# Latent attention rebuilt: keys and values first, two heads per unit in paired tiles, queries grouped by part

## The reference, cut to what matters

```
cq, ckv, k_rope = split(h @ w_down, [256, 384])            # 256 | 128 | 32 columns
q  = (rms_norm(cq)  @ w_uq ).reshape(b, s, 16, 64 + 32)    # q_nope, q_rope
kv = (rms_norm(ckv) @ w_ukv).reshape(b, s, 16, 64 + 64)    # k_nope, v
q_rope, k_rope = apply_axial_rope(...)                     # latent tokens only
s = (q_nope . k_nope + q_rope . k_rope) * 96 ** -0.5       # 16 heads, 256 queries, 512 keys
y = (softmax(s) @ v) @ w_o
```

## Time and profile before

| quantity | value |
|---|---|
| median of 3 runs | 3352.78 us (3351.43 to 3356.87) |
| the profiled execution, on the device | 3355.39 us |
| its span, first to last instruction | 3354.1 us |
| TensorE busy | 3137.0 us, 94% of the span |
| VectorE busy | 1747.7 us, 52% |
| ScalarE busy | 1449.1 us, 43% |
| GpSimd busy | 995.2 us, 30% |
| mean granted TensorE clock | 0.974 of full speed |

### The profile page before, as it was taken

The page is one execution under the profiler, slowest core; times in us unless marked ns, Lnnn a source line. Parts: engine busy times, 40 slices in busy tenths (PEclk is TensorE's granted clock), DMA queues, the critical chain, the costliest instruction groups (busy, mean ns, idle before and its releaser), DMA issues.

```text
span 3354.1 us, 50677 instructions
## 1 busy us (share of the span) xinstructions
PE 3137.0 (94%) x21050; PEld 2666.3 (79%) x21050; DVE 1747.7 (52%) x3034; ACT 1449.1 (43%) x2412; POOL 995.2 (30%) x440
## 2 busy tenths in 40 slices
PE   5989998999899998889979989999999999999899
PEld 3767776776677775569979977877999978779899
DVE  3353333655543333756556646555456556654565
ACT  3442222444432223544454445555444446554443
POOL 0312222110212222123433432333444433434433
PEclk8999999999899999999989989999999999999999
DMA  8345444332355552125525532333545433334454
GB/s 289 121 143 163 157 159 137 126 101 89 121 173 171 168 171 90 38 63 178 193 91 164 188 116 89 101 101 94 166 143 183 157 115 96 99 101 151 151 177 151
DMA packets 469299, 459.97 MB, mean 137 GB/s; under 512 B 9040, under 2 KB 467664, under 8 KB 469072
## 3 DMA queue, kind: packets, MB, share of 16 engines
q1 hardware_dynamic: 465760, 453.32, 42.4%
q10 hardware_dynamic: 3312, 3.42, 0.3%
HBM read 455.66 MB, written 1.05 MB: 136 GB/s over the span
## 4 chain that ended last, share of the span: by engine, by line
PE 77%; DVE 11%; ACT 7%; issue 3%; POOL 1%; DMA 1%; ACTq 0%; DVEq 0%; POOLq 0%
PE bank L399 22%; PE bank L400 21%; PE bank L401 21%; PE bank L443 3%; ACT wh L346 3%; DVE wl L362 2%; DVE hl L707 1%; PE bank L1474 1%; PE bank L1465 1%; PE bank L2212 1%; PE bank L457 1%; PE bank L1016 1%; DVE bc L2252 1%; PE bank L1178 1%; DVE tmp L595 1%
## 5 line engine op out<-in xcount | busy, mean ns | idle before, releaser
L374 POOL TENSOR_TENSOR wl<-raw,wh 128x768 fp32r<-128x768 f32 (+1 forms) x336 | 877.2, 2611 | 2177.7 <-ACT wh L346 2167.7
L346 ACT ACTIVATE wh<-raw 128x2048 fp32r<-128x2048 f32 x336 | 636.4, 1894 | 318.9 <-PE bank L401 315.4
L362 DVE TENSOR_TENSOR wl<-raw,wh 128x1280 fp32r<-128x1280 f32 (+1 forms) x336 | 500.4, 1489 | 419.7 <-ACT wh L346 410.6
L399 PE MATMUL bank<-nh,wh 128*128 128x272 f32 (+1 forms) x1712 | 510.9, 298 | 23.5 <-DVE nl L1797 22.8
L401 PE MATMUL bank<-nh,wl 128*128 128x272 f32 (+1 forms) x1712 | 497.7, 291 | 0.0
L400 PE MATMUL bank<-nl,wh 128*128 128x272 f32 (+1 forms) x1712 | 496.7, 290 | 0.0
L399 PE MATMUL bank<-xh,wh 128*128 128x512 f32 (+2 forms) x1264 | 445.3, 352 | 45.2 <-ACT xh L563 24.7
L400 PE MATMUL bank<-xl,wh 128*128 128x512 f32 (+2 forms) x1264 | 437.0, 346 | 0.0
L401 PE MATMUL bank<-xh,wl 128*128 128x512 f32 (+2 forms) x1264 | 435.8, 345 | 0.0
L399 PEld LDWEIGHTS bank<-nh,wh 128*128 128x128 f32 x1712 | 331.0, 193 | 40.0 <-issue 37.8
L399 PE MATMUL bank<-hh,wh 128*128 128x512 f32 (+1 forms) x1024 | 350.3, 342 | 3.7 <-DVE X L615 1.9
(11 more groups left out here) (414 smaller groups left out, 5675.5 us busy)
## 6 DMA issues: line engine op xcount, KB each, us to landing
raw<-in_mlp_w SPq DMA_DIRECT2D x128, 1024.0 KB, 5.3
raw<-in_mod_w SPq DMA_DIRECT2D x83, 1024.0 KB, 5.2
raw<-in_w_in SPq DMA_DIRECT2D x60, 1024.0 KB, 5.2
raw<-in_w_mlp_up SPq DMA_DIRECT2D x32, 1024.0 KB, 5.7
raw<-in_w_mlp_down SPq DMA_DIRECT2D x32, 1024.0 KB, 5.2
raw<-in_w_in SPq DMA_DIRECT2D x34, 512.0 KB, 4.3
raw<-in_w_ssd_down SPq DMA_DIRECT2D x16, 1024.0 KB, 5.1
early<-in_mod_w SPq DMA_DIRECT2D x13, 1024.0 KB, 11.9
```

Of the source, the lines that this page charges most:

```text
L346: nc.scalar.activation(self.wtile(self.wh, c1), self.rawtile(c1), AF.Copy).then_inc(*up("act_wh", ("wh", c1)))
L362: nc.vector.tensor_tensor(l, r, h.bitcast(F32), ALU.subtract).then_inc(*up("dve_wl", ("wl_dve", c1)))
L374: nc.gpsimd.tensor_tensor(l, r, h.bitcast(F32), ALU.subtract).then_inc(*up("pool_wl", ("wl_pool", c1)))
L399: nc.tensor.matmul(o, ah, bh, start=first, stop=False)
```

## The change

- The weights of the two up projections are reordered on the host (`by_part`): within each half of eight heads, first the 64-wide parts of all eight, then the other parts. The chunks of the layer come in another order: the second down chunk (ckv and rope columns) first, then the first (cq), both `ukv` chunks, both `uq` chunks.
- Down projection: ckv (128 columns) and the rope columns (now a group of 32) over 512 tokens, then cq over the 256 latent tokens only, since only they have queries.
- The norm chain is split in two: one for ckv (512 columns), started between the two cq groups, and one for cq (256 columns). Products are read straight from PSUM. The rotated rope rows of the keys are made once and replicated to four groups of 32 partitions by eight small matmuls.
- All keys (eight groups, each two heads) and all values (eight groups of 512 columns) are made before the attention. Queries: eight groups of 128 rows for the 64-wide parts, four of 128 rows for the rope parts of four heads each. Rope is four matmuls with three VectorE instructions each instead of 16. Six of the twelve query groups and two of the ropes are issued within the first steps of the attention.
- The attention has one loop of 16 units; a unit is two heads (i) and 128 queries, in steps s = 0 to 18. Scores: for each head one matmul over 64 rows (the two heads in upper and lower rows of the array), then one over 32 rows (the rope part), both into bank 2 + i. There is one pair of score banks, 2 and 3; banks 0 and 1 serve the queries and the output projection.
- GpSimd scales the second head's exponentials, VectorE the first's. Values: eight matmuls of 64 stationary and 128 moving columns, the two heads alternating in left and right columns of the array.
- In steps 16 and 17 TensorE does six eighths of the first two groups of `mwo`.

```diff
+        for i in range(6):
+            self.pe_mla_query(i, RING)
+        for s in range(19):
+            self.pe_mla_step(s)
+            if s < 6:
+                self.pe_mla_query(6 + s, (0, 1))
+            if s == 6:
+                self.pe_mla_rope(3)
+            if s in (16, 17):
+                self.pe_mwo(s - 16, 0, 6)
+        for g in range(8):
+            self.pe_mwo(g, 6 if g < 2 else 0, 8)
...
+    def pe_mla_step(self, s):
+        nc, at, up, PE = self.nc, self.T.at, self.T.up, self.PE
+        u = s - 2
+        if 0 <= u < 16:
+            for i in range(2):
+                b = self.pe_bank((4 + i,), "mt", u, i)
+                PE.wait_ge(*at("mp", u, i))
+                for t in range(4):
+                    ins = nc.tensor.transpose(b[:, 128 * t:128 * t + 128], self.mE[u % 3][:, i, 128 * t:128 * t + 128], self.ident[:])
+                ins.then_inc(*up("pe_turned", ("acc", "mt", u, i)))
+        if s < 16:
+            p, q = s // 2, s % 2
+            qs = slice(128 * q, 128 * q + 128)
+            bs = [self.pe_bank((2 + i,), "ms", s, i) for i in range(2)]
...
+            for i, b in enumerate(bs):
+                r = slice(64 * i, 64 * i + 64)
+                nc.tensor.matmul(b[:], self.mQN[r, p, qs], self.mKN[r, p, :], start=True, stop=False)
+            for i, b in enumerate(bs):
+                r = slice(32 * ((2 * p + i) % 4), 32 * ((2 * p + i) % 4) + 32)
+                nc.tensor.matmul(b[:], self.mQR[r, p // 2, qs], self.mKR[r, :], start=False, stop=True).then_inc(*up("pe_scores", ("acc", "ms", s, i)))
+        u = s - 3
+        if 0 <= u < 16:
...
+            for t in range(4):
+                for i in range(2):
+                    ins = nc.tensor.matmul(b[64 * i:64 * i + 64, 128 * q:128 * q + 128], self.mV[:, t, 128 * p + 64 * i:128 * p + 64 * i + 64],
+                                           self.mPT[u % 2][:, 4 * i + t, :], start=(t == 0), stop=(t == 3))
+            ins.then_inc(*up("pe_values", ("acc", "mo", u)))
...
     def dve_mla_step(self, s):
+        if s < 16:
+            mx, nm, ac, r = self.dstats(s)
+            for i in range(2):
+                DVE.wait_ge(*at("acc", "ms", s, i))
+                nc.vector.tensor_reduce(mx[:, i:i + 1], self.place["ms", s, i][:], AX, ALU.max).then_inc(*DVE.step())
...
+            nc.vector.tensor_scalar(nm, mx, -(96 ** -0.5), None, ALU.mult).then_inc(*up("dve_mmax", ("mmax", s)))
+        u = s - 2
+        if 0 <= u < 16:
...
+            nc.vector.tensor_copy(self.mPT[u % 2][:, 4:8, :], self.place["mt", u, 1][:].rearrange("p (s q) -> p s q", q=128)
...
+        if s < 16:
+            E = self.mE[s % 3][:, 0, :]
+            DVE.wait_ge(*at("me", s))
+            nc.vector.reciprocal(r, ac).then_inc(*up("dve_mr", ("mr", s)))
+            DVE.wait_ge(*at("mr", s))
+            nc.vector.tensor_scalar(E, E, r[:, 0:1], None, ALU.mult).then_inc(*up("dve_mp", ("mp", s, 0)))
...
     def act_mla(self):
+        self.act_split(self.ix["down", 1])
+        self.act_latent_square(0)
...
+        self.act_latent_root(0)
+        self.act_latent_square(1)
...
+        self.act_latent_high(0)
+        self.act_latent_root(1)
+        self.act_latent_high(1)
         self.act_split(self.ix["down", 0])
+        self.act_split(self.ix["ukv", 0])
         for hf in range(2):
             self.act_split(self.ix["ukv", hf])
+            for p in range(4):
+                ACT.wait_ge(*at("acc", "mk", 4 * hf + p))
+                nc.scalar.activation(self.mKN[:, 4 * hf + p, :], self.place["mk", 4 * hf + p][:], AF.Copy
...
     def pool_mla(self):
+        for s in range(16):
+            E, r = self.mE[s % 3][:, 1, :], self.dstats(s)[3]
+            POOL.wait_ge(*at("mr", s))
+            nc.gpsimd.tensor_tensor(E, E, r[:, 1:2].broadcast_to([128, 512]), ALU.mult).then_inc(*up("pool_mp", ("mp", s, 1)))
```

More of the change, by code:

```diff
@@ L1403, in mla_memory @@
[L1403 to L1407, removed]
+        self.mQN = self.tiles("mqn", 8, 256, F32, o)
+        self.mQR = self.tiles("mqr", 4, 256, F32, o + 8192)
+        self.mKN = self.tiles("mkn", 8, 512, F32, o + 12288)
+        self.mV = self.tiles("mv", 4, 1024, F32, o + 28672)
@@ L1416, in pe_mla @@
[L1416 to L1427, removed]
@@ L1483, in pe_mla @@
[L1483 to L1491, removed]
+        hi, lo = self.pe_take(c)
+        os = [(self.pe_bank((0,), "md", 0)[:], slice(0, 128)), (self.pe_bank((1,), "md", 1)[0:32, :], slice(128, 160))]
@@ new lines, in pe_mla, with pe_latent @@
+        for i in range(6):
[10 more added lines that the diff above has]
+            self.pe_mwo(g, 6 if g < 2 else 0, 8)
+    def pe_latent(self, u):
+        nc, at, up, PE = self.nc, self.T.at, self.T.up, self.PE
+        keys, T, g, dim, parts = self.latent(u)
+        b = self.pe_bank((4 + u,), "mtot", u)
+        for n in range(len(keys)):
+            PE.wait_ge(*at("msq", u, n))
+            ins = nc.tensor.matmul(b[:, T], self.ones[:], self.tmp[u + n][:, T], start=(n == 0), stop=(n == len(keys) - 1))
+        ins.then_inc(*up("pe_acc", ("acc", "mtot", u)))
@@ L1556, in act_mla @@
+        self.act_split(self.ix["uq", 0])
+        for i in range(6):
+            self.act_mla_query(i)
+        self.act_split(self.ix["uq", 1])
+        for s in range(19):
+            self.act_mla_step(s)
+            if s < 6:
+                self.act_mla_query(6 + s)
         square = None
@@ L1631, in dve_mla @@
-        for j in range(4):
-            self.dve_split(self.ix["mwo", j])
-            for m in range(2):
-                self.dve_resid(("mwo", 2 * j + m), 2, 2, 2 * j + m, LAT, "mlp2")
-    def pool_mla(self):
-        for c in range(self.ix["down", 0], self.ix["mwo", 0]):
-            self.pool_split(c)
+        for n, key in enumerate(keys):
+            nc.vector.scalar_tensor_tensor(out=self.tmp[u + n][:, T], in0=self.place[key][:, T], scalar=self.col(g, n), in1=rs[:], op0=ALU.mult, op1=ALU.mult
+                                           ).then_inc(*up("dve_mct", ("mct", u, n), ("out", *key)))
@@ L2700, in constants @@
     rt[:, 0:256], rt[:, 256:512] = np.tile(cos, (2, 1)), np.tile(sin, (2, 1))
-    rt[64:96, 512:768], rt[64:96, 768:1024] = rope(32)
+    rt[:, 512:768], rt[:, 768:1024] = (np.tile(x, (4, 1)) for x in rope(32))
     c["rt1"] = rt.astype(f)
```

398 lines of the change are left out of this document (217 added, 181 removed).

## The result

The changed kernel takes 3384.29 us in the median of 4 runs (3383.55 to 3386.39), the kernel before 3353.36 (3351.43 to 3356.87) beside it. The ratio is 1.0092, with a 95% interval of 1.0075 to 1.011: 31 us slower, where 22.9 us faster was forecast. The profiled execution has a span of 3383.4 us (3354.1 before) and a mean granted clock of 0.964 (0.974).

What follows compares the result with a forecast made beforehand. TensorE was taken as the old loop's bound (4.61 us a unit), score banks as the new one's (5.15). Savings around the loop end the layer at 1468.5 instead of 1491.4, 22.9 us earlier: from the median 3329.9, forecast 3330, range 3317 to 3348.

Steps and rivals of the forecast that it cites:

- Down projection and norm chain: Before the keys: cq part 5.1 us less TensorE work; keys can start at 1331.7, not 1346; cq ready at 1338.6.
- Keys and values: Before the queries: 10.9 us of matmuls instead of 16.3, with TensorE idle most of 1333 to 1341.3.
- ScalarE's splits stand before its key copy at their own length: Before the first key copy: two highs and two chunk splits (1.05 and 1.5 us) on ScalarE; copy ends at 1341.3.
- Scores and values: TensorE's loop work: scores 1.95 us together, values 0.95, transposes 0.93; sum 3.8 us a unit, less than 4.61.
- The rival of unpaired 32-row tiles: In the loop's scores: 32-row tiles don't pair, scores 2.9 us, period 6.05, total 3346; chance 0.14.
- The loop: Attention, 16 units: 5.15 us a unit, paced by one pair of score banks; last exponentials ready at 1442.0.
- TensorE's other work fits into the 3.2 us between: Within a loop unit: transposes 0.93, values 0.95 and a query 0.73 in the first six steps fit between scores.
- on VectorE copy and low part lie under the 1.51 us wait for the exponentials: VectorE in a loop unit: copy and low part (0.68 + 0.45 us) are hidden in that wait.
- Half clock: Rival in the loop: clock lost, TensorE's 3.83 us become 7.7, 38 us more, total 3368; chance 0.08.
- the ring: Loop's serial chain of scores, maxima, exponentials, then next scores through one pair of banks: 5.15 us a unit.
- The tail: After the last exponentials (1442.0): remaining values, transposes and `mwo` matmuls, 153 of them 18.5 us; end 1468.4 + 0.1.
- The 1.2 us forecast for ropes: In the loop: two ropes in steps 2 and 6 don't quite fit, adding 1.2 us.

Runs made afterwards that it cites:

- Run 4: Changed kernel with the first and second `uq` chunks swapping raw weight buffers, so the first needs none just left by the second `ukv` chunk: 3377.79 us.
- Run 3: Changed kernel with ScalarE's copy of the old transposed block before the exponentials, VectorE's copy and low part before the maxima: 3344.50 us.
- Run 5: Changed kernel, order untouched, plus unused filler matmuls on TensorE before the transposes and before the values in odd steps: 3374.07 us.
- run 2: Changed kernel with only VectorE's low part of two finished units' output moved before the maxima of the step: 3364.78 us.
- run 6: Changed kernel with the first four key and value copies before the split of the first `uq` chunk, buffers as they were: 3381.82 us.
- run 7: Changed kernel with the edits of runs 3, 4 and 6 together: 3338.59 us, ratio 0.9952.
- run 8: Run 7 plus second score banks in even steps from 6, scores issued before transposes, VectorE's reciprocal and scaling behind the next unit's maxima: 3330.86 us.

## Why the prediction was wrong

The forecast was 3330 and the range 3317 to 3348; 3384.3 lies 54 us above the one and 36 above the other. All three signs of being wrong that it named came: a period above 6, a clock that fell within the loop, and scores that were not what waits there. By its own steps:

- *Down projection and norm chain*: right. Keys were to start at 1331.7 in the old clock, 1329.8 in this one; they started at 1330.03.
- *Keys and values*: the stall for cq in banks 2 and 3 was there (2.78 us). **The step that failed is the one where ScalarE's splits stand before its key copy at their own length.** The second of them was taken to have its data. In the new chunk order its raw buffer is the one that the second `ukv` chunk lies in, so SyncE could issue the load only when GpSimd's share of that split was done (1339.09). (In the kernel before, the first `uq` chunk took over the buffer of a down chunk.) Run 4 prices it at 6.5 us. The prediction followed the splits and never asked which buffer each load needs.
- *Scores and values*: right in mechanism, and the 3.8 us a unit were 4.16 (1.06 + 1.06 + 1.02 + 1.02). The rival of unpaired 32-row tiles is out.
- *The loop*, the larger part: **the step that failed is "TensorE's other work fits into the 3.2 us between", with its reason, "on VectorE copy and low part lie under the 1.51 us wait for the exponentials".** It summed durations and found room. It didn't ask when the banks come free. The copies lie under that wait only because they stand behind the maxima, and TensorE's transposes and values, which stand ahead of the next scores, wait for just these copies. The chain is: scores, maxima, exponentials, copy of the old block, transposes, next scores, 6.75 us. ScalarE's copy wasn't in the sum at all. Run 3, with nothing but the order changed, gives the step as forecast, 5.34 for 5.15, with the scores released by the exponentials.
- *Half clock*: a rival with 0.08, priced as if the ring stayed 5.15. It came on top of a longer ring: 1.8 us a step (8.54 against 6.75); the earlier trace rows had shown the clock falling behind a wait. Its break-even, a period of 6.7, was close to what the order alone makes. Run 5 shows it with the order untouched, run 2 with the same step.
- *The tail*, from the last exponentials to the layer's end, was 6.8 us longer: the transposes and values there ran in part at half clock and waited for the same copies. (The forecast counted 153 remaining matmuls of `mwo`, where 192 less 36 are 156, 0.4 us.)

The balance, counted from the layer's first matmul: the first exponentials came 7.3 us later than forecast, from there to the last ones it took 42.6 more, and the tail 6.8 more, 56.7 in all. (The rest of the program was 4.4 us shorter in this trace than in the one before; over all the traces it varies by 6 us.) Of the 54.3 us between forecast and median, run 3 takes back 39.8 (order and clock together; runs 2 and 5 put the clock's part at 10 to 20, the order's at the rest), runs 4 and 6 in its company 5.9. The layer of run 7 is then 170.9 us, where 162.8 were forecast. Of these 8.1, 0.7 lie before the first exponentials and 0.7 in the tail. The others are in the loop: 0.19 a step is 2.9, the three steps behind the first, 7.30, 6.09 and 6.23 with the clock at 0.77, are 3.6 longer than 5.34. The 1.2 us forecast for ropes came too, in one step of 6.56. So the change as such gains; the order in which it emptied its buffers lost more than that.

## What to carry to other kernels

When a loop is modelled as a ring, follow every buffer around it, not only the one with the new value: for each wait of the bound engine, find the instruction that empties the buffer, and what stands ahead of that in its engine's list. An instruction that frees something old belongs before the wait for something new. And when the order of weight chunks changes, list which buffer each chunk inherits, and from whom.

## What the runs showed of the hardware

- Two kernels with the same work and the same step of 6.75 us at full clock got different clocks. In run 2, with a wait of 2.5 us in every step, the clock fell once and then stayed at 2.4 GHz (1.00 over 27.02 us). In the changed kernel, with two such waits in the odd step and none in the even one, as much in sum, it went up and down between 1.2 and 2.4 GHz through 77 us. The Trainium skill, TensorE: Matmul & The Clock Gate, section on psum-queue depth-cycling, says that small idle gaps between groups of matmuls, when a kernel cycles through PSUM banks, can make the clock oscillate, told of a bf16 kernel; the changed kernel's trace agrees (0.68 over 76.9 us), runs 2 and 3, with waits of 2.5 and 1.1 us in every step, don't show it for most of their loops. Why the one order recovers and the other doesn't stays open; no run isolates it.
- Pairs in 32 rows of plain float32 cost 1.05 us, as much as pairs in 64 rows (1.06), with the change of form between them included.
- VectorE's scaling with one operand in SBUF takes 1.37 us when GpSimd's of 1.04 us starts with it, and 0.49 alone. The Trainium skill, SBUF — State Buffer, section on the two separate sides, says that the pair of ports that the two share is held for a whole instruction and the other engine blocks, where VectorE works in a mode that uses that pair. The runs fit this: in run 8 VectorE's scaling ends 0.29 us behind GpSimd's, as if it did most of its 0.49 after it. Its record starts 0.04 us ahead of GpSimd's, so the records don't tell which took the ports first, and whether GpSimd's 1.04 would be less alone wasn't tried.
